# Two reduced-precision products in place of one full fp32 product for the stick-breaking scores

## The reference, cut to what matters

```python
q, k, v = heads(q), heads(k), heads(v)          # (B, 8, T, 64), T = 512
z = jnp.einsum('bhqd,bhkd->bhqk', qb, k).astype(jnp.float32) * scale
mask = kpos[None, :] < tq[:, None]
log_rem = jnp.where(mask, jax.nn.log_sigmoid(-z), 0.0)
suffix = lax.cumsum(log_rem, axis=3, reverse=True) - log_rem
a = jnp.where(mask, jnp.exp(jax.nn.log_sigmoid(z) + suffix), 0.0)
return jnp.einsum('bhqk,bhkd->bhqd', a, v)
```

## Time and profile before

| | us |
|---|---|
| median of 3 runs | 1870.87 (1869.71 to 1872.06) |
| the profiled execution | 1871.18, its span 1869.4 |
| PE busy | 1831.7 (98% of the span) |
| DVE busy | 1152.4 (62%) |
| ACT busy | 770.4 (41%) |
| POOL busy | 466.5 (25%) |
| stick-breaking, first score to last value product | 1332.4 to 1403.8 |
| NSA attention before it | 1230.5 to 1332.6 |
| the mixer's projections before that | 1079.1 to 1230.6 |

### The profile page before, as it was taken

The page is one execution under the profiler, slowest core; times in us unless marked ns, Lnnn a source line. Parts: engine busy times, 40 slices in busy tenths (PEclk is TensorE's granted clock), DMA queues, the critical chain, the costliest instruction groups (busy, mean ns, idle before and its releaser), DMA issues.

```text
span 1869.4 us, 29612 instructions
## 1 busy us (share of the span) xinstructions
PE 1831.7 (98%) x12020; PEld 1631.1 (87%) x12020; DVE 1152.4 (62%) x1677; ACT 770.4 (41%) x1392; POOL 466.5 (25%) x322
## 2 busy tenths in 40 slices
PE   8999999999999999999999999999999999999999
PEld 8999888979988887899988877989768878999887
DVE  7533465555416657999984555646556579999631
ACT  4122455311235644444433324445564644444331
POOL 5443211354341122000034423320003420000343
PEclk9999999999999999999999999999999999999999
DMA  4322000222220012432322223200003213323132
GB/s 165 97 84 91 35 12 13 80 90 103 80 90 2 23 46 80 140 109 91 102 74 94 98 102 126 86 24 1 1 1 120 84 57 126 115 99 103 69 100 102
DMA packets 41048, 145.49 MB, mean 78 GB/s; under 512 B 5072, under 2 KB 5328, under 8 KB 40784
## 3 DMA queue, kind: packets, MB, share of 16 engines
q1 hardware_dynamic: 40912, 143.59, 22.5%
HBM read 140.40 MB, written 2.10 MB: 76 GB/s over the span
## 4 chain that ended last, share of the span: by engine, by line
PE 87%; DVE 7%; ACT 3%; issue 2%; DMA 1%; POOL 0%; SPq 0%; DVEq 0%; ACTq 0%
PE ps L470 22%; PE ps L471 22%; PE ps L472 22%; PE ps L1066 6%; PE ps L1097 5%; PE ps L1082 2%; PE ps L2675 1%; PE ps L2658 1%; ACT wh L446 1%; DVE xl L560 1%; DVE XSl L1691 1%; PE ps L2416 1%; PE ps L2646 1%; PE ps L1276 1%; DMA raw<-wstream 1%
## 5 line engine op out<-in xcount | busy, mean ns | idle before, releaser
L454 POOL TENSOR_TENSOR wl<-raw,wh 128x1024 fp32r<-128x1024 f32 (+1 forms) x170 | 411.7, 2422 | 1032.8 <-ACT wh L446 1032.7
L446 ACT ACTIVATE wh<-raw 128x1024 fp32r<-128x1024 f32 (+1 forms) x178 | 188.5, 1060 | 604.7 <-PE ps L472 533.1
L470 PE MATMUL ps<-xh,wh 128*128 128x264 f32 (+3 forms) x1144 | 384.4, 336 | 9.5 <-DVE wl L466 3.4
L471 PE MATMUL ps<-xl,wh 128*128 128x264 f32 (+3 forms) x1144 | 380.8, 333 | 0.0
L472 PE MATMUL ps<-xh,wl 128*128 128x264 f32 (+3 forms) x1144 | 380.3, 332 | 0.0
L470 PE MATMUL ps<-XSh,wh 128*128 128x256 f32 (+1 forms) x864 | 284.2, 329 | 5.7 <-DVE wl L1749 3.7
L471 PE MATMUL ps<-XSl,wh 128*128 128x256 f32 (+1 forms) x864 | 284.1, 329 | 0.0
L472 PE MATMUL ps<-XSh,wl 128*128 128x256 f32 (+1 forms) x864 | 283.6, 328 | 0.0
L470 PEld LDWEIGHTS ps<-xh,wh 128*128 128x128 f32 x1144 | 215.2, 188 | 37.6 <-issue 7.3
L471 PEld LDWEIGHTS ps<-xl,wh 128*128 128x128 f32 x1144 | 215.3, 188 | 22.4 <-issue 1.0
L472 PEld LDWEIGHTS ps<-xh,wl 128*128 128x128 f32 x1144 | 215.4, 188 | 21.9
(11 more groups left out here) (419 smaller groups left out, 3470.1 us busy)
## 6 DMA issues: line engine op xcount, KB each, us to landing
raw<-wstream SPq DMA_DIRECT2D x176, 512.0 KB, 3.3
rawx<-wpairs SPq DMA_DIRECT2D x44, 512.0 KB, 3.5
raw<-wpairs SPq DMA_DIRECT2D x24, 512.0 KB, 3.5
raw<-wstream SPq DMA_DIRECT2D x10, 528.0 KB, 3.4
h<-xT SPq DMA_DIRECT2D x4, 528.0 KB, 6.2
out<-h SPq DMA_DIRECT2D x8, 256.0 KB, 4.3
xs<-wpairs SPq DMA_DIRECT2D x2, 512.0 KB, 4.5
HF<-wpairs SPq DMA_DIRECT2D x2, 512.0 KB, 5.4
```

The costliest lines, as they stand in the source:

```text
L446: e.activation(wh[p % 2][:, 0:n], raw[c % 2][:, 0:n], ACT.Copy).then_inc(*w_hi(p))
L454: e.tensor_tensor(wl[p % 2][:, 0:n], raw[c % 2][:, 0:n], wh[p % 2][:, 0:n].bitcast(F32), ALU.subtract).then_inc(*w_lo(p))
L470: e.matmul(o, w_h, x_h, start=start, stop=False)
L471: e.matmul(o, w_h, x_l, start=False, stop=False)
```

## The change

- `QS` and `KS` become fp32r. `QS[:, a, :]` now holds head a's high part on the head's own 64 rows and its low part on the other 64, where the zeros were. `break_key(a)` holds the high part of head a's keys on both halves of the rows, so that one product over 128 rows gives high·high plus high·low. `break_key_low(c)` holds the keys' low parts of two heads, and a second product, over the head's 64 rows, gives low·high.
- Room: `KS` has the high keys of heads 0 to 3. Those of heads 4 to 7 lie in the weight buffers `wh` of key tiles 2 and 3. The low keys lie in the new `KSL` for tiles 0 and 1, and in `wl` for tiles 2 and 3. So the splits of `wout2` chunks 0 and 1 move from the `ks` tiles to the end of stick-breaking, behind the last scores that read those buffers.
- DVE writes the scaled tile to `tmpn[:, c % 2]`. For each tile ACT makes the high parts from it: two 64x512 copies for `qs`, four for `ks`; DVE makes the low parts: two 64x512 subtractions. The eight memsets of `QS` go.

```diff
-        QS = sb("QS", [128, 8, T], at=two)
-        KS = sb("KS", [128, 4, T], at=two)
+        QS = sb("QS", [128, 8, T], F32R, at=two)
+        KS = sb("KS", [128, 4, T], F32R, at=two)
+        KSL = sb("KSL", [128, 2, T], F32R, at=two)
...
+        def break_key(a):
+
+            if a < 4:
+                return KS[:, a, :]
+            return wh[PART["ks", a // 2] % 2][:, T * (a % 2):T * (a % 2) + T]
+
+        def break_key_low(c):
+
+            return KSL[:, c, :] if c < 2 else wl[PART["ks", c] % 2][:, 0:T]
+
+        def break_high_act(e, on, key):
+            kind, c = key
+            on.wait_ge(*v_out[key])
+            for g, (p0, p1) in enumerate(((0, 64), (64, 128))):
+                src = tmpn[p0:p1, c % 2, 0:T]
+                if kind == "qs":
+                    r = e.activation(QS[p0:p1, 2 * c + g, :], src, ACT.Copy)
+                else:
+                    e.activation(break_key(2 * c + g)[p0:p1], src, ACT.Copy)
+                    r = e.activation(break_key(2 * c + g)[64 - p0:128 - p0], src, ACT.Copy)
+            r.then_inc(*a_out(*key, "high"))
+
+        def break_low_dve(e, on, key):
+            kind, c = key
+            on.wait_ge(*a_out[key + ("high",)])
+            for g, (p0, p1) in enumerate(((0, 64), (64, 128))):
+                src = tmpn[p0:p1, c % 2, 0:T]
+                if kind == "qs":
+                    dst, high = QS[64 - p0:128 - p0, 2 * c + g, :], QS[p0:p1, 2 * c + g, :]
+                else:
+                    dst, high = break_key_low(c)[p0:p1], break_key(2 * c + g)[p0:p1]
+                r = e.tensor_tensor(dst, src, high.bitcast(F32), ALU.subtract)
+            r.then_inc(*v_lo(*key))
...
@@ mix_act
+                else:
+                    break_high_act(e, on, key)
...
+            for c in range(2):
+                split_hi(e, on, PART["ks", c] + 2)
             for c in range(4):
-                split_hi(e, on, PART["ks", c] + 2)
+                break_high_act(e, on, ("ks", c))
@@ mix_dve
-            for k in range(8):
-                a = 64 * (1 - k % 2)
-                e.memset(QS[a:a + 64, k, :], 0.0)
...
+                    if j and MIX[j - 1][0] == "qs":
+                        break_low_dve(e, on, MIX[j - 1])
...
-                    for a in (0, 64):
-                        w = e.scalar_tensor_tensor(QS[a:a + 64, 2 * c + a // 64, :], src[a:a + 64, :], 0.125,
-                                                   r[a:a + 64, :], ALU.mult, ALU.mult)
+                    if c >= 2:
+                        on.wait_ge(*v_lo["qs", c - 2])
+                    e.scalar_tensor_tensor(tmpn[:, c % 2, 0:T], src, 0.125, r, ALU.mult, ALU.mult).then_inc(*v_out(*key))
...
                 on.wait_ge(*tile["ks", c])
-                e.tensor_tensor(KS[:, c, :], PS[:, 512 * bank["ks", c]:512 * bank["ks", c] + T], rst[:, 0:T],
+                on.wait_ge(*(v_lo["ks", c - 2] if c >= 2 else v_lo["qs", c + 2]))
+                e.tensor_tensor(tmpn[:, c % 2, 0:T], PS[:, 512 * bank["ks", c]:512 * bank["ks", c] + T], rst[:, 0:T],
                                 ALU.mult).then_inc(*v_out("ks", c))
+                if c:
+                    break_low_dve(e, on, ("ks", c - 1))
+            break_low_dve(e, on, ("ks", 3))
@@ mix_pool
-            parts_pool(e, on, ("kc", 0), ("ks", 3))
+            parts_pool(e, on, ("kc", 0), ("ks", 1))
@@ sb_pe
-                on.wait_ge(*v_out["ks", 3])
-                e.matmul(ps[:, 0:T - q0], KS[:, a // 2, q0:q0 + 128], QS[:, a, q0:T], start=True, stop=False)
+                p0 = 64 * (a % 2)
+                on.wait_ge(*a_out["ks", 3, "high"])
+                on.wait_ge(*v_lo["ks", 3])
+                e.matmul(ps[:, 0:T - q0], break_key(a)[:, q0:q0 + 128], QS[:, a, q0:T], start=True, stop=False)
+                e.matmul(ps[:, 0:T - q0], break_key_low(a // 2)[p0:p0 + 64, q0:q0 + 128], QS[p0:p0 + 64, a, q0:T],
+                         start=False, stop=False)
@@ sb_act
+                    if t_ == 3:
+                        on.wait_ge(*score["sb", 7, 0])
+                        split_hi(e, on, PART["wout2", 1])
                     on.wait_ge(*pv["sb", a])
...
                     e.activation(xh[:, 4 + t_, M:L], fin[:, f, 0:T], ACT.Copy).then_inc(*x_hi("ao", "sb", t_))
+                    if t_ == 2:
+                        on.wait_ge(*score["sb", 5, 0])
+                        split_hi(e, on, PART["wout2", 0])
@@ sb_pool
+                if t_ == 3:
+                    split_lo(e, on, PART["wout2", 0])
+                    split_lo(e, on, PART["wout2", 1])
```

More of the change, by code:

```diff
@@ L2355, in mix_dve @@
                     on.wait_ge(*tile[key])
-                    on.wait_ge(*v_one["zeros"])
-                    for a in (0, 64):
-                        w = e.scalar_tensor_tensor(QS[a:a + 64, 2 * c + a // 64, :], src[a:a + 64, :], 0.125,
-                                                   r[a:a + 64, :], ALU.mult, ALU.mult)
-                    w.then_inc(*v_out(*key))
+                    if c >= 2:
+                        on.wait_ge(*v_lo["qs", c - 2])
+                    e.scalar_tensor_tensor(tmpn[:, c % 2, 0:T], src, 0.125, r, ALU.mult, ALU.mult).then_inc(*v_out(*key))
                 if j in (3, 7):
```

## The result

The changed kernel took 1887.5 us (median of 4 runs, 1882.8 to 1890.0) against 1870.8 (4 runs, 1869.7 to 1872.1): a ratio of 1.0086, with a 95% interval of 1.0064 to 1.0108. It is slower, as forecast, but by 16.7 us and not by 4.8, and it lies outside the range of 1868.8 to 1878.3.

What follows compares the result with a forecast made beforehand. PE's (TensorE's) work was taken as the bound, 87% of the chain. Stick-breaking +3.2, NSA start +2.3 and mixer -0.7 gave +4.8 us on 1871.18, so 1876.0; less 0.3, 1875.7 us; 8-of-10 range 1868.8 to 1878.3.

Steps and rivals of the forecast that it cites:

- NSA start: Start of the NSA attention: ACT's copies and DVE's subtractions of the last key tile delay the first transpose, +2.3 us.
- the rivals: Four alternatives: 64 rows cost nothing extra, 0.25; NSA start hidden, 0.08; detour costs 0.38, 0.12; first two together, 0.05.
- Detour: Stick-breaking scores: going from 128 rows to the second product's 64 and back costs PE 0.30 us a score.
- Rival C: Stick-breaking scores: the detour costs 0.38 us, +2.2 us, total 1877.9; chance 0.12.
- Rival A: Stick-breaking scores: 64 rows cost nothing extra, so scores save 0.87 us a head, total 1869.5; chance 0.25.
- the signs that the forecast named: Changed profile: mask product 0.76 us after a 512-column high product begins, PEld idle before 64-row load, first NSA transpose later.
- Narrow products: Stick-breaking scores: products of 128 and of 256 columns were each taken to hold PE 0.12 us.
- Stick-breaking: First scores +0.7, two two-head cycles +1.1, split after head 5 +1.0, POOL's low part holding DVE +0.4: +3.2 us.
- Mixer: Mixer's start: dropping DVE's `QS` memsets removes a PE wait, -0.8 us; projections +0.1; together -0.7 us.

Runs made afterwards that it cites:

- experiments 1 to 4: Changed kernel: last key tile's work deferred, 1879.7 us; PE's wait filled, 1880.0. Kernel before: ACT and DVE delay added, 1884.2; delay with filling, 1874.8.
- experiment 6: Changed kernel with each score's second product on all 128 rows instead of one head's 64: 1878.8 us, ratio 1.0040.
- experiment 12: Changed kernel with the last key tile's copies and subtractions deferred into the NSA attention and the eight `QS` memsets put back: 1881.5 us, ratio 1.0052.
- Experiment 7: Changed kernel, 64-row products kept, last key tile's work in later NSA units, six filling products on PE at stick-breaking's start: 1876.5 us, ratio 1.0028.
- experiment 2: Changed kernel with nine unused 128x512 products on PE just ahead of its first NSA transpose: 1880.0 us, ratio 1.0041.
- experiment 3: Kernel before with only the delay added ahead of the first NSA unit (four ACT copies, two DVE subtractions): 1884.2 us, ratio 1.0061.
- experiment 9: Changed kernel with 128-row second products, late key tile copies and the first weight chunk's split in head 6, no filling products: 1869.6 us, ratio 0.9992.

## Why the prediction was wrong

The direction and most of the mechanisms were right, and the sum failed above all at one sentence: "The granted clock is 1.00 throughout" was read from two stretches of the kernel before and carried over to the changed one, so the price of a fall stood at nothing in the sum.

- **NSA start, +2.3 forecast.** The lateness itself was right: +2.24. What was missing is what PE's wait does to the clock: another 7.85 us, shown from both sides by experiments 1 to 4. This is the step that failed. None of the rivals had it, though the fall at 960 in the kernel before was there to be read.
- **Detour, 0.30 forecast, 0.40 measured.** The rows of 32-row products were used as if their price held for 64 rows between fp32r products. Rival C, at 0.38, was the closest. Rival A, that 64 rows are like 128, is out: experiment 6 has the same product on 128 rows, 0.29 to 0.39 us a score cheaper. Of the signs that the forecast named, the idle time before the 64-row load is there (0.45 us), and the mask product starts 0.66 us behind the high one and not 0.76, since half of the detour lies in the mask product itself.
- **Narrow products, 0.12 forecast for 128 columns, 0.06 measured** for the high one. I had taken the distance of short products bound by something else as a floor. It cancelled a part of the detour's error.
- **Stick-breaking, +3.2 forecast, +4.09 measured.** By heads: +0.52 up to the first values and +0.56 for the next head (forecast together 0.7), +0.84 for each of the two cycles (0.55), +1.33 for the one with the split (1.4), in which POOL's low part, from 1404.67 to 1407.03, held DVE's copy from 1406.12 to 1407.10.
- **Mixer, -0.7 forecast, +0.1 measured.** Counted from DVE's first work there, PE was 0.75 us earlier at 1092 and 0.2 earlier at 1129, and the difference at the end, +0.1, is within what executions differ by (experiment 12). I had priced the wait that goes, and not asked what is late next, which was the arrival of weights.
- **The run-to-run spread.** Profile against profile the loss is 14.7 us, of the medians 16.7; the runs at 0.991 and 0.992 were longer than the profiled one at 0.994. By these clocks the length of the low stretch differs from run to run.

Without the clock's 7.85 us the changed kernel's stages come to +6.8, and the forecast was +4.8: the rest is stick-breaking's 0.9 and the mixer's 0.8, with 0.3 from ahead of the mixer. Experiment 7's seven undisturbed spans, 1873.6 to 1875.8, lie around the forecast's 1869.4 + 4.8 = 1874.2, but that is luck: the kernel there doesn't have the +2.3 at the NSA attention, and two terms that were too low make up for it. The nearest to a test is experiment 2's run at a clock of 1.00, whose span of 1873.6 is one run alone.

The Trainium skill names the risk. TensorE: Matmul & The Clock Gate, in "Loop structure matters more than you think", says that products must follow each other closely to keep the clock, and that waits between bursts lose it. The traces agree, by the rows at 0.50 behind the wait of 2.08 us. Its example is a wait for a DMA ahead of every product; that one wait for ACT is enough is what the rows here add. TensorEngine Tiling (Array Packing), "Key Properties", says that a change of the tiling mode drains TensorE; the 0.40 us agrees with it.

## What to carry to other kernels

A wait on the bound engine has two prices: its length, and what it does to the clock afterwards. Here 2 us of waiting cost 10 to 13 at the start of the NSA attention, and a wait as long at 957 us cost far less beyond its own length, with 3.4 us at half clock or none. Idle time can be filled with products that nobody reads if real work can't be moved. So read the granted clock by stretch, in the profile before as well as in the changed one, and when a change adds a wait of PE of the length seen here, give a fall of the clock a chance and a price of its own.
When a product needs only half of the rows, compare it with one over all 128 rows whose other half adds nothing that matters, as here a product of two low parts; between 128-row neighbours it may be the cheaper one.
Before a stall is booked as a gain, follow the next arrival of weights: whatever waits for DMA can take it back.

## What the runs showed of the hardware that I had not expected

- PE at full busy share and half clock: 19.00 us busy of 19.00 at 0.50. It fell after 2.08 us without work, and stayed for 20 us of unbroken work in one case, 30 us in another (experiment 3), and 3 to 4 us in others (at 960 in the kernel before, at 1337 in experiment 9).
- The same program has the fall in some runs and not in others: by the mean clocks 2 of 9 in experiment 7. Behind the wait at 957 it came in 9 of 14 traces, with the same instructions up to there.
- A 64-row fp32r product between 128-row ones costs 0.19 to 0.20 us on the way in and as much on the way out, at all four widths.
- A DVE copy of 128x128 from SBUF to SBUF took 1.93 us beside a POOL subtraction, 0.23 alone. I had priced only the addition of two SBUF tensors so the earlier trace rows. The Trainium skill's GPSIMD Engine Reference, section "1. Specifications", names DVE instructions in a two-port mode beside those with two SBUF inputs. The trace agrees in that a copy was held; in which mode it ran, no run here shows.
